# Spatial gating in a three-block kernel: the position bias moved from VectorE into the matmul's accumulation, the PSUM copy from ScalarE to VectorE

## The reference

```
def spatial_gating(xn, w_in, ln_g, ln_b, sgu_w, sgu_b, w_out):
    """Chunked causal gMLP: (u * (W_s LN(v) + b)) W_out over chunks of CHUNK positions."""
    z = jax.nn.gelu(xn @ w_in, approximate=False)
    u, v = jnp.split(z, 2, axis=-1)
    v = layer_norm(v, ln_g, ln_b)
    ...
    mask = jnp.tril(jnp.ones((CHUNK, CHUNK), dtype=bool))
    ws = jnp.where(mask[None], sgu_w, jnp.zeros_like(sgu_w))
    mixed = jnp.einsum('gts,bnsgc->bntgc', ws.astype(v.dtype), vc)
    mixed = mixed + jnp.transpose(sgu_b)[:, :, None].astype(v.dtype)
    mixed = mixed.reshape(bsz, s, SGU_WIDTH)
    return (u * mixed) @ w_out
```

## Time and profile before

| | |
|---|---|
| median of three runs | 4507.35 us (4506.37 to 4509.85) |
| the profiled execution | 4509.85 us, its span 4508.1 us |
| TensorE matmul busy | 3942.9 us, 87% |
| VectorE busy | 2244.8 us, 50% |
| ScalarE busy | 1285.5 us, 29% |
| `SpatialGate`, first scaling to first matmul of `Narrow` | 2404.10 to 2428.70 us |

### The profile page before, as it was taken

How to read it: one execution, slowest core, us unless ns; L and a number is a source line. 1 busy time by engine, 2 the same in 40 slices (tenths; PEclk the granted TensorE clock), 3 DMA queues, 4 the chain that set the end, 5 groups by cost and what they waited for, 6 DMA issues and landing times. The chain is left out here.

```text
span 4508.1 us, 54166 instructions
## 1 busy us (share of the span) xinstructions
PE 3942.9 (87%) x20801; PEld 3124.2 (69%) x20801; DVE 2244.8 (50%) x3393; ACT 1285.5 (29%) x1787; POOL 0.2 (0%) x4
## 2 busy tenths in 40 slices
PE   7799999978999898799987899673799957998998
PEld 6567887767788784588865788572577734676886
DVE  3475555344556534543354534446666646425344
ACT  2353333221333313222233322223111122223222
POOL 0000000000000000000000000000000000000000
PEclk9899999975999997899999999885899967899998
DMA  3102222210222220122221222120000000022221
GB/s 125 56 0 75 94 93 95 92 47 0 84 93 93 86 93 19 47 93 94 93 84 47 75 93 93 62 73 0 5 0 0 0 19 19 11 84 78 98 93 66
DMA packets 43493, 278.97 MB, mean 62 GB/s; under 512 B 5935, under 2 KB 6831, under 8 KB 10740
## 3 DMA queue, kind: packets, MB, share of 16 engines
q1 hardware_dynamic: 36576, 266.35, 16.6%
q10 hardware_dynamic: 6804, 11.05, 0.7%
HBM read 275.28 MB, written 2.11 MB: 62 GB/s over the span
## 5 line engine op out<-in xcount | busy, mean ns | idle before, releaser
L213 PE MATMUL PS<-XH,WH 128*128 128x512 f32 (+1 forms) x2704 | 1041.7, 385 | 27.3 <-DVEq L95 23.5
L214 PE MATMUL PS<-XL,WH 128*128 128x512 f32 (+1 forms) x2704 | 1043.3, 386 | 0.0
L215 PE MATMUL PS<-XH,WL 128*128 128x512 f32 (+1 forms) x2704 | 1037.8, 384 | 0.0
L146 DVE TENSOR_TENSOR WL<-W,WH 128x2048 fp32r<-128x2048 f32 x254 | 582.2, 2292 | 890.7 <-ACT WH L136 885.1
L136 ACT ACTIVATE WH<-W 128x2048 fp32r<-128x2048 f32 x254 | 485.6, 1912 | 1230.7 <-PE PS L303 683.1
L213 PEld LDWEIGHTS PS<-XH,WH 128*128 128x128 f32 x2704 | 510.0, 189 | 145.8 <-issue 20.2
L214 PEld LDWEIGHTS PS<-XL,WH 128*128 128x128 f32 x2704 | 509.2, 188 | 109.0 <-issue 2.2
L215 PEld LDWEIGHTS PS<-XH,WL 128*128 128x128 f32 x2704 | 510.5, 189 | 104.6
L301 PE MATMUL PS<-HH,WH 128*128 128x512 f32 (+1 forms) x1024 | 401.7, 392 | 10.5 <-DVEq L95 9.3
L484 DVE TENSOR_TENSOR PS<-PS,R 128x512 f32<-128x512 f32 x248 | 171.5, 697 | 466.2 <-PE PS L215 465.7
L302 PE MATMUL PS<-HL,WH 128*128 128x512 f32 (+1 forms) x1024 | 399.7, 390 | 0.0
(11 more groups left out here) (445 smaller groups left out, 5163.7 us busy)
## 6 DMA issues: line engine op xcount, KB each, us to landing
W<-in_weights SPq DMA_DIRECT2D x254, 1024.0 KB, 4.8
X<-in_x ACTq DMA_DIRECT2D x1, 2048.0 KB
out<-X ACTq DMA_DIRECT2D x1, 2048.0 KB, 7.1
consts<-in_consts ACTq DMA_DIRECT2D x1, 1026.0 KB
bias<-bias_spread ACTq DMA_DIRECT2D x4, 256.0 KB
w_gd<-in_w_gd ACTq DMA_DIRECT2D x1, 640.0 KB
rope<-in_c_rope ACTq DMA_DIRECT2D x1, 528.0 KB
ws<-in_ws ACTq DMA_DIRECT2D x1, 512.0 KB
```

The lines of the kernel that those rows point to most:

```text
L146: P.e.tensor_tensor(K.WL[:, s, :], K.W[:, s, :], K.WH[:, s, :].bitcast(F32), ALU.subtract).then_inc(P.sem("weights_split"), P.adds("weight ...
L213: P.e.matmul(out, wh[:, k, c], xh[:, k, r], start=(k == 0), stop=False)
L214: P.e.matmul(out, wh[:, k, c], xl[:, k, r], start=False, stop=False)
L215: last = P.e.matmul(out, wl[:, k, c], xh[:, k, r], start=False, stop=(k == KT - 1))
```

## The change

On TensorE each matmul of M(t) leaves its accumulation open, and a second one follows into the same 128x128 piece of PSUM: weights are one row of 128 ones (one partition), the moving operand is the group's bias as one row. It adds the bias to every channel. On VectorE the addition and its wait are gone, and the product with u reads PSUM directly. The copy to `s_vT` moves from ScalarE to VectorE. The wait that keeps M(t) from overwriting a bank goes from `sgu_biased` to `sgu_gated`. `sgu_b` becomes a tile on one partition, and its load is no longer broadcast to 128.

```
 VectorE (dve)
             if t + 2 < KT:
                 scaled(t + 2)
+            if t < KT:
+                P.e.wait_ge(P.sem("sgu_transposed"), P.due("sgu_transposed"))
+                P.e.tensor_copy(K.s_vT[:, t % 2, :], K.PS[:, t % 2, :]).then_inc(P.sem("sgu_vT"), P.adds("sgu_vT"))
             if 1 <= t <= KT:
-                v = K.v2[:, t - 1, :]
-                bias = K.sgu_b[:, t - 1, :].rearrange("p (a n) -> p a n", a=1).broadcast_to([128, 4, 128])
                 P.e.wait_ge(P.sem("sgu_mixed"), P.due("sgu_mixed"))
-                P.e.tensor_tensor(v.rearrange("p (a n) -> p a n", a=4), K.PS[:, 2 + (t - 1) % 2, :].rearrange("p (a n) -> p a n", a=4), bias, ALU.add).then_inc(P.sem("sgu_biased"), P.adds("sgu_biased"))
-                P.e.wait_ge(P.sem("sgu_biased"), P.due("sgu_biased", 0))
-                P.e.tensor_tensor(v, v, K.u2[:, t - 1, :], ALU.mult).then_inc(P.sem("sgu_gated"), P.adds("sgu_gated"))
+                P.e.tensor_tensor(K.v2[:, t - 1, :], K.PS[:, 2 + (t - 1) % 2, :], K.u2[:, t - 1, :], ALU.mult).then_inc(P.sem("sgu_gated"), P.adds("sgu_gated"))
 ScalarE (act)
-            if 1 <= t <= KT:
-                P.e.wait_ge(P.sem("sgu_transposed"), P.due("sgu_transposed"))
-                P.e.activation(K.s_vT[:, (t - 1) % 2, :], K.PS[:, (t - 1) % 2, :], ACT.Copy).then_inc(P.sem("sgu_vT"), P.adds("sgu_vT"))
 TensorE (pe)
                 if t >= 3:
 
-                    P.e.wait_ge(P.sem("sgu_biased"), P.due("sgu_biased"))
+                    P.e.wait_ge(P.sem("sgu_gated"), P.due("sgu_gated"))
                 for n in range(4):
                     c = slice(128 * n, 128 * n + 128)
                     out = K.PS[:, 2 + (t - 1) % 2, c]
-                    last = P.e.matmul(out, K.s_vT[:, (t - 1) % 2, c], K.ws[:, t - 1, :], start=True, stop=True)
+                    P.e.matmul(out, K.s_vT[:, (t - 1) % 2, c], K.ws[:, t - 1, :], start=True, stop=False)
+                    last = P.e.matmul(out, K.one_row2[0:1, 0:128], K.sgu_b[0:1, t - 1, :], start=False, stop=True)
 tiles and loads
-        ... v("sgu_b", [128, 8, 128], 5248), K.ones_row
+        ... v("sgu_b", [1, 8, 128], 5248), K.ones_row
-            ... (K.sgu_b[:, :, :], args["sgu_b"].partition_broadcast(128))]
+            ... (K.sgu_b[0:1, :, :], args["sgu_b"])]
-        arrays["sgu_b"] = a["sgu_b_2"][0]
+        arrays["sgu_b"] = a["sgu_b_2"]
```

More of the change, by code:

```diff
@@ L2595, in program @@
         K.u2, K.v2 = K.uv2[:, 0:8, :], K.uv2[:, 8:16, :]
-        K.ws, K.sgu_b, K.one_row2 = v("ws", [128, 8, 128], 4224), v("sgu_b", [128, 8, 128], 5248), K.ones_row
+        K.ws, K.sgu_b, K.one_row2 = v("ws", [128, 8, 128], 4224), v("sgu_b", [1, 8, 128], 5248), K.ones_row
         K.s_vT = v("s_vT", [128, 2, S], 6272)
@@ L2668, in program @@
                         (K.onehot[:, :], args["onehot"])]
-            K.loads2b = [(K.ws[:, :, :], args["ws"]), (K.sgu_b[:, :, :], args["sgu_b"].partition_broadcast(128))]
+            K.loads2b = [(K.ws[:, :, :], args["ws"]), (K.sgu_b[0:1, :, :], args["sgu_b"])]
         stages = [Prologue()]
```

## The result

The changed kernel is slower: 4536.77 us median (4535.25 to 4537.7) against 4507.33 us (4506.37 to 4509.85) on the same chip, ratio 1.0065 with a 95% interval of 1.0053 to 1.0078. The forecast was 4540.

The account below looks back on a forecast made before the run. VectorE was taken to bound the middle of the stage before, TensorE after, with 6.67 us rounds at the low clock. Narrow moves from 2428.70 to 2461.4, 32.7 us, giving 4540; range 4534 to 4544 at 0.76.

Parts of the forecast that it names:

- M(t) = 8 x 0.7225 = 5.78 us: TensorE, a tile's mixing and bias matmuls: eight of alternating row count, 0.7225 us each at the low clock.
- 0.50 for the whole stage: TensorE's granted clock stays at the low level, 1.2 GHz, throughout SpatialGate, where before it rose after some 4 us.
- rival A: TensorE's clock rises early as before, 0.413 us a matmul: 11.3 us more, 4518.7; chance 0.14 with a rise midway.
- The 0.16 us for a change at the high level: TensorE: each change of row count between matmuls adds 0.16 us at the high clock, 0.28 at the low one.
- Rival B: TensorE: a single row costs no switch, M(t) takes 2.0 us and the time stays at 4507; chance 0.08.
- The copy, the bank wait and the smaller load: VectorE's copy costs 0, at most 0.1 us; the bank wait 0; the bias load cost 0, gain 0.
- for the transposes in each round: Sign of a right forecast: VectorE waits for M and for TensorE's transposes in every round of the stage.
- 32.7 forecast: Whole kernel: Narrow, the next stage, starts at 2461.4 instead of 2428.70, 32.7 us later.

Follow-up runs that it names:

- e3_wide_row: Changed kernel with one one-row bias matmul of 512 columns ahead of the four mixing ones, instead of four of 128; stage 28.11 us, 4511.27 us, ratio 1.0011.
- e4_warm: Changed kernel with seven 128-row filler matmuls before the stage's first transpose, so it opens at the high clock; stage 54.40 us, 4538.23 us, ratio 1.0071.
- e2_grouped: Changed kernel with each tile's four mixing matmuls first, then its four one-row bias matmuls; stage 26.50 us, 4513.08 us, ratio 1.0017.
- e1_full_rows: Changed kernel with bias matmuls of 128 rows (1/128 weights, broadcast bias) instead of one row; stage 24.68 us, 4509.39 us, ratio 1.0006.
- e9_half_rows: Changed kernel with bias matmuls of 64 rows instead of one, adding half the bias; stage 56.65 us, 4544.75 us in one run.
- e10_pairs: Changed kernel with each tile's matmuls ordered two mixing, two bias, two mixing, two bias; stage 47.13 us, 4534.76 us, ratio 1.0053.
- e8_full_rows_act_warm: Changed kernel with 128-row bias matmuls, the copy back on ScalarE and ten 128-row fillers; stage 23.50 us, 4508.56 us, ratio 0.9998.
- e7_before_warm: Kernel before the change with ten 128-row filler matmuls around the stage; stage 23.26 us, 4504.71 us, ratio 0.9995, and 0.9994 when run again.

## Why the prediction was right

- The step that carries the sum, "M(t) = 8 x 0.7225 = 5.78 us", taken from 64-row matmuls, held: 0.7225 us a matmul for one row and for 64. M(0) took 5.78 us. In the six full rounds the first matmul of M, which follows T, took 0.56, so that M(t) was 5.63 and the round 6.54 instead of 6.67. Over the stage the forecast was 57.3 us, measured 56.62.
- "0.50 for the whole stage" held. The reasons given were too weak. One was that M(0) begins to take turns 1.8 us after the first transpose; e3_wide_row has its first change 1.87 us after it, and its level rose. The other, that taking turns keeps a low level low, is true of this order, and e4_warm shows more, that it brings a high one down. It opened high and still took 54.40 us, against the 36 of rival A (2404.10 to 2440.0). The window at 1.00 that spoke for A is of wider matmuls with runs of 128-row ones between. What parted the runs here is the count of changes: with two a tile the level rose (e3_wide_row) and stayed (e2_grouped), with four and with eight it did not rise. Whether four a tile would keep a level that is already high was not tried.
- The 0.16 us for a change at the high level was 0.413 us less 0.25 taken from the transposes. e1_full_rows has 0.22 us for a matmul without a change, so that a change costs 0.19 to 0.20 us where every matmul takes turns; in e2_grouped it is 0.16.
- Rival B fell in e9_half_rows and e1_full_rows. The Trainium skill, "TensorEngine Tiling (Array Packing)", Key Properties, says that a change of tiling mode drains TensorE; the trace agrees in the price, with 0.16 us for a change at the high level (e2_grouped) and 0.72 instead of 0.43 us a matmul at the low one. Equal time for few and many rows, as "TensorE: Matmul & The Clock Gate" of the Trainium skill has it in the table of "Why this matters for your kernels", holds for matmuls in a row (e2_grouped), not for ones that take turns.
- The copy, the bank wait and the smaller load cost nothing, as said. In the changed kernel no matmul waited for the copy or the bank; one weight load waited 0.3 us for the copy. In e1_full_rows, which keeps the copy and the bank wait but has the broadcast load, the stage is 24.68. The smaller load was not tried alone, but e2_grouped has it: its stage is 1.8 us longer than e1_full_rows's, and 16 changes at 0.16 us, 2.6 us, more than cover that.
- One sign did not come: VectorE was to wait "for the transposes in each round". It waited for them once, 0.8 us, ahead of the first copy; all its other waits of the stage's rounds are for M, 35.0 us.
- The sum went 3 us too far in the whole: 32.7 forecast, 29.4 measured between medians. The stage took 0.7 of them less; `Narrow` opened at the low level for 3.5 us instead of 4.9, about 0.7 us less. The rest, about 2 us, is within what parts of the kernel that weren't changed vary by: between the two profiled executions the changed one starts the stage 2.4 us earlier (2401.72 instead of 2404.10) and takes 4.0 us less behind it. That 4540 came so near has some luck in it.

## What to carry to other kernels

Matmuls over one row in between full ones are not free: price each change of row count, in both directions, and put matmuls of one kind together; here the order alone is worth 30 us of stage. If a bias must be added in the accumulation, a full-height constant such as 1/128 against a broadcast bias avoids the change. And ask whether the clock holds before pricing at the high level: a change costs 0.16 to 0.20 us there and 0.26 to 0.29 at the low one, and every matmul between goes from 0.22 to 0.43 us.

## What the runs showed of the hardware

- TensorE's granted clock fell from 1.00 to 0.50 inside M(0), where the records show TensorE busy without a gap (e4_warm), and stayed at 1.00 where the same place had 128-row matmuls alone (e8_full_rows_act_warm). A busy share of 100% in the profile doesn't mean that the clock is kept.
- Between two and four changes of row count a tile the stage went from 26.50 to 47.13 us (e2_grouped, e10_pairs).
- Fillers of 128 rows in the idle time kept the level at 1.00 across the 3.5 us before `Narrow` where it had fallen to 0.50 (e7_before_warm). Where the idle time is shorter, the same fillers hold up what comes next: 0.6 us in e8_full_rows_act_warm.
